# Last projection of a two-block transformer kernel: products ordered by token tile and by half of the contraction, final norm by tile, store in four parts

## Chip, core and metric

The kernel runs as one program on one core of a Trainium2 chip. The metric is device time in microseconds (us), the median of the runs; lower is better. The engines named below are TensorE (PE in the rows; PEld is its weight load), VectorE (DVE), ScalarE (ACT), GpSimd (POOL) and SyncE (SP), which here issues nearly all DMAs.

## What is computed

256 tokens of width 1024 pass through two blocks in float32. The first is a gated recurrence beside latent attention and then a mixture of 64 experts; the second has three attentions (moba, dsa, cross), a gated merge of their outputs and an output projection. Only the end of the second block matters here:

```python
def hybrid_layer(x, mem, ...):
    ...
    gates = jax.nn.sigmoid(glog + b_merge).reshape(B, S, N_BRANCH_2, D_MODEL)
    u = gates[:, :, 0] * ya + gates[:, :, 1] * yb + gates[:, :, 2] * yc
    return x + u @ w_out                      # u: 256 x 1024, w_out: 1024 x 1024

def rmsnorm_2(x, g):
    xf = x.astype(jnp.float32)
    y = xf * lax.rsqrt(jnp.mean(xf * xf, axis=-1, keepdims=True) + RMS_EPS)
    return (y * g.astype(jnp.float32)).astype(x.dtype)

# second_block returns rmsnorm_2(x, g_final)
```

## The kernel before

The 256 tokens are two tiles of 128 (NT = 2), and the width of 1024 is 8 pieces of 128 (KC = 8). `X` holds the residual stream with tokens on the partitions, `[128, 2, 1024]`. The order of all work is one list, `PLAN`, made by `plan()` and written out by hand. Each engine has its own program that walks this list and issues its own part of each step, so the order on an engine is the order of the list; between engines there are only semaphores.

Matrix products go to four regions of PSUM of 1024 columns: `P0` and `P1`, which the `proj` steps use in turn, and `A` and `B`. `full[r]` counts how often a region has been filled, `empty[r]` how often it has been read out. `may_fill` makes TensorE wait until the region's previous use was read. `USE` keeps these counts for each step.

The last steps of the list are `um0, um1, ud0, ud1, ux0, ux1` (the three branches' up-projections, feature-major, each half of the 1024 features: index 0 is features 0 to 511, index 1 features 512 to 1023), then `w20, w21` (the output projection, columns 0 to 511 and 512 to 1023) and `final`.

- After each `ux` step VectorE multiplies the result by its gate and adds it to `gl[0]`, two operations; the second frees the region. `gl[0]` is `u` transposed, `[128, 8, 256]`: pieces 0 to 3 are complete after `ux0`, 4 to 7 after `ux1`.
- `w20` and `w21` (`token_major`, L803 by way of `proj`) take a 128 x 128 piece of `gl[0]` as weights and 512 columns of `w_out` as the moving operand. Both wait until `ux0` and `ux1` have been read out (L932 to L935). Each does token tile 0 over the eight pieces, then token tile 1 over the eight. In float32 each product is two matmul records in the trace: 8 x 2 x 2 = 32 for each of `w20` and `w21`. One semaphore increment stands at the end of each.
- VectorE adds the region to `X`, both token tiles in one operation of 1024 columns (the line of `tt`, L1298).
- `final`: ScalarE squares both tiles with a sum over the row (L1099), loads the table of the square root and takes it (L1102). VectorE takes the reciprocal (L1305) and multiplies each tile by the root and by the gain row (L1681). SyncE then stores the whole output, 1 MB, with one DMA (L775), and waits for it.

Weights come into a ring of four slots; those of `w21` go to the slot of `um` and are issued when `um1` is done.

Of the kernel before, what the change touches and what calls it, by code (L numbers as in the profile page):

```python
# [141 lines left out]
def plan():  # L142
# [3 lines left out]
    def proj(*names):  # L146
        p.extend(("proj", n, "P") for n in names)
# [74 lines left out]
    turn(5, 9, "gl4")  # L222
    turn(9, 10, "gl5")
    turn(10, None, "um0", "um1")
    proj("ud0", "ud1", "ux0", "ux1", "w20", "w21")
    p.append(("final", 0, ""))
    return p


# [37 lines left out]
def build(nc, ins, out):  # L267
    with ExitStack() as ctx:
# [131 lines left out]
        def one_up(e, name):  # L400
            for s in ONE_UP[name]:
                e.sem_inc(s, 1)
        stored = sem("stored")

        block = ctx.enter_context(nc.Block())

# [303 lines left out]
        def _(sp):  # L710
# [60 lines left out]
                    sp.dma_start(wrow_f, ins["g_final_2"].unsqueeze(0).broadcast_to([P, D])).then_inc(row_in, 16)  # L771
                load(UNITS_2, n)

            sp.wait_ge(normed, 5)
            sp.dma_start(out[0].rearrange("(t p) d -> p t d", p=P), xo[:, :, :]).then_inc(stored, 16)  # L775
            sp.wait_ge(stored, 16)


        @block.gpsimd
# [8 lines left out]
        def _(pe):  # L788
            def transposes(key, src_of, region, n, done=True):
# [3 lines left out]
                    mm = pe.transpose(ps[region][:, i * P:(i + 1) * P], src_of(i), ident)  # L793
                mm.then_inc(full[region], 1)

            def proj(key, name, lhs_of, rhs_of, kc, outs):

                may_fill(pe, key)
                r = region_of(key)
                for o in range(len(outs(ps[r]))):  # L800
                    dst = outs(ps[r])[o]
                    for k in range(kc):
                        mm = pe.matmul(dst, lhs_of(o, k), rhs_of(o, k), start=(k == 0), stop=(k == kc - 1))  # L803
                mm.then_inc(full[r], 1)

            def rows_out(cols):
                return lambda z: [z[:, t * 512:t * 512 + cols] for t in range(NT)]
# [14 lines left out]
            rope_n = {"iq": 1, "ik": 1, "dq": 2, "dk": 3, "mq": 4, "mk": 5}  # L822

            for name, arg, _ in PLAN:
                key = (name, arg)
                if name == "norm":
                    if arg == "x":
# [49 lines left out]
                elif name == "proj":  # L877
# [23 lines left out]
                    elif arg in ("wa0", "wa1"):  # L901
                        if arg == "wa0":
                            wait_empty(pe, ("hg_outT", 0))
                        feature_major(key, arg, oaT)
                    elif arg in ("wb0", "wb1"):
                        if arg == "wb0":
                            wait_empty(pe, ("pv", 2))
                        feature_major(key, arg, obT)
                    elif arg == "wo0":
                        wait_empty(pe, ("proj", "wb0"))  # L910
                        wait_empty(pe, ("proj", "wb1"))
                        token_major(key, arg, Y)
                    elif arg in ("iq", "dq", "dk", "dv", "mq", "mk", "mv"):
                        if arg == "iq":
                            wait_empty(pe, ("norm", "mid"))
                        token_major(key, arg, hT)
                    elif arg == "ikw":
                        token_major(key, arg, hT, cols=72)
                    elif arg in ("xq", "mg", "dg", "xg") or arg[:2] == "gl":
                        feature_major(key, arg, hT)  # L920
                    elif arg == "xk":
                        wait_empty(pe, ("norm", "mem"))
                        feature_major(key, arg, memT)
                    elif arg == "xv":
                        token_major(key, arg, memT)
                    elif arg[0] == "u":
                        kind = {"m": "mg", "d": "dg", "x": "xg"}[arg[1]]
                        last = {"m": 8, "d": 5, "x": 10}[arg[1]]
                        if arg[2] == "0":
                            wait_empty(pe, ("pv", last))  # L930
                        feature_major(key, arg, sg[kind], kc=4, c0=512 * int(arg[2]))
                    elif arg in ("w20", "w21"):  # L932
                        if arg == "w20":
                            wait_empty(pe, ("proj", "ux0"))
                            wait_empty(pe, ("proj", "ux1"))  # L935
                        token_major(key, arg, gl[0])
                elif name == "level":
                    n = arg
# [142 lines left out]
        def _(act):  # L1081
# [31 lines left out]
            for name, arg, _ in PLAN:  # L1113
# [165 lines left out]
                elif name == "moe":  # L1279
                    rounds = moe_scalar(act)  # L1280
                elif name == "final":
                    wait_empty(act, ("proj", "w20"))
                    wait_empty(act, ("proj", "w21"))
                    square_sums(lambda t: X[:, t, :], lambda t: xo[:, t, :], 4, 48, D)


        @block.vector
        def _(dve):
# [68 lines left out]
            for name, arg, _ in PLAN:  # L1357
# [63 lines left out]
                elif name == "proj":  # L1421
# [36 lines left out]
                    elif arg == "wo1":  # L1458
# [1 line left out]
                        tt(X[:, 0, 512:D], ps[r][:, 0:512], X[:, 0, 512:D], ALU.add).then_inc(x_sum, 1)  # L1460
                        wait_full(dve, key)
                        tt(X[:, 1, 512:D], ps[r][:, 512:1024], X[:, 1, 512:D], ALU.add).then_inc(empty[r], 1)
                    elif arg in ("wo0", "w20", "w21"):
                        i = int(arg[2])
                        wait_full(dve, key)
                        x = tt(X[:, :, 512 * i:512 * i + 512], rows(ps[r]), X[:, :, 512 * i:512 * i + 512], ALU.add)
# [205 lines left out]
                elif name == "moe":  # L1672
                    rounds = experts(dve, link, tt)
                elif name == "final":

                    wait_empty(dve, ("proj", "w20"))
                    wait_empty(dve, ("proj", "w21"))
                    inverse_root(50)
                    dve.wait_ge(row_in, 32)
                    for t in range(NT):  # L1680
                        i = dve.scalar_tensor_tensor(out=xo[:, t, :], in0=X[:, t, :], scalar=small[:, 50 + t:51 + t],  # L1681
                                                     in1=wrow_f, op0=ALU.mult, op1=ALU.mult)
                    i.then_inc(normed, 1)

# [54 lines left out]
```

## Time and profile before

| | us |
|---|---|
| median of 3 runs | 1761.36 |
| lowest, highest | 1760.98, 1761.41 |
| the profiled execution's own time | 1762.46 |
| its span in the profile | 1760.6 |
| PE busy | 1384.9 (79%) |
| DVE busy | 329.5 (19%) |
| ACT busy | 209.0 (12%) |

The span runs from the first to the last instruction that the profiler recorded; the 1.86 us between it and the execution's own time lie around it. "Busy" is a share of the whole span and says little about one stage: the expert stage, from about 430 to 1350 us, is bound by its weights' transfers, and the end of the program by a chain of single instructions. The chain that ended last (below) gives for each step what released it. The granted clock is the share of TensorE's full 2.4 GHz that it was given in a stretch: 1.00 is 2.4 GHz, 0.50 is 1.2 GHz, and a value between them is a mean over both.

### The profile page before, as it was taken

The page shows a single profiled execution, that of the slowest core. Times are in us where ns is not written, and L with a number is a line of the kernel's source. Part 1 is how long each engine was busy: PE and PEld are TensorE (multiplying, and loading weights), DVE is VectorE, ACT ScalarE, POOL GpSimd, SP SyncE. Part 2 cuts the span into 40 slices and gives each one's busy share as a digit, 9 for nine tenths or more (in the row PEclk, how much of TensorE's full clock was granted, in tenths as well). Part 3 has the DMA queues.
Part 4 walks back from the last instruction along what each step waited for, and adds up shares of the span by engine and source line. Part 5 has one row for each costly group of instructions (what it writes and reads, how often), then busy time and mean ns, then how long its engine had stood idle before and what let it go on. Part 6 is the DMA issues. An engine that isn't in the chain of part 4 may idle for free.

```text
span 1760.6 us, 16409 instructions
## 1 busy us (share of the span) xinstructions
PE 1384.9 (79%) x7184; PEld 778.7 (44%) x7184; DVE 329.5 (19%) x585; ACT 209.0 (12%) x366; POOL 1.4 (0%) x6
## 2 busy tenths in 40 slices
PE   6999989888866676656666666666667999999996
PEld 5756886775322122212221222122214546788882
DVE  2233432312211001101010101010101221252221
ACT  1000032202000000000000000000001001143300
POOL 0000000000000000000000000000000000000000
PEclk9999998988987788878887888888878999999998
DMA  7324133317999999999999999999997433332310
GB/s 285 114 103 172 67 117 146 102 51 330 394 429 433 433 431 429 433 434 432 429 430 435 433 429 430 435 433 430 430 435 337 171 134 137 132 144 108 142 50 24
DMA packets 24550, 504.43 MB, mean 287 GB/s; under 512 B 4672, under 2 KB 4928, under 8 KB 6336
## 3 DMA queue, kind: packets, MB, share of 16 engines
q1 hardware_dynamic: 24080, 503.69, 68.6%
q8 instruction: 30, 0.49, 0.1%
q10 hardware_dynamic: 432, 0.17, 0.0%
q14 instruction: 8, 0.07, 0.0%
HBM read 502.81 MB, written 1.05 MB: 286 GB/s over the span
## 4 chain that ended last, share of the span: by engine, by line
PE 51%; DMA 44%; DVE 3%; ACT 1%; issue 1%; SPq 0%; DVEq 0%; ACTq 0%
DMA arena<-in_experts 44%; PE psP L803 35%; PE psP L481 5%; PE psP L492 3%; DVE arena L1298 2%; PE psB L1064 1%; PE psB L793 1%; PE psA L948 1%; PE psB L948 1%; PE psA L1030 1%; PE psA L1029 1%; PE psA L793 0%; PE psA L502 0%; PE psP L848 0%; PE psP L842 0%
## 5 line engine op out<-in xcount | busy, mean ns | idle before, releaser
L803 PE MATMUL psP<-arena,ring 128*128 128x256 f32 x1664 | 369.3, 384 | 2.2 <-DVE arena L1298 1.4
L803 PEld LDWEIGHTS psP<-arena,ring 128*128 128x128 f32 x1664 | 319.1, 193 | 48.1 <-issue 4.2
L481 PE MATMUL psP<-ring,arena 128*32 128x512 f32 x1024 | 162.1, 792 | 103.9 <-DMA ring<-in_experts 103.9
L803 PE MATMUL psP<-ring,arena 128*128 128x512 f32 (+2 forms) x576 | 233.1, 564 | 7.3 <-DVE arena L1298 7.3
L481 PE MATMUL psP<-arena 128*32 128x512 f32 x1024 | 158.1, 774 | 99.8 <-DMA arena<-in_experts 99.8
L1298 DVE TENSOR_TENSOR X<-X,psA 128x512 f32<-128x512 f32 x68 | 46.8, 688 | 682.1 <-PE psA L502 682.1
L803 PEld LDWEIGHTS psP<-ring,arena 128*128 128x128 f32 x576 | 105.7, 191 | 126.1 <-issue 126.0
L481 PEld LDWEIGHTS psP<-ring,arena 128*32 128x32 f32 x1024 | 41.0, 139 | 223.2 <-issue 176.5
L481 PEld LDWEIGHTS psP<-arena 128*32 128x32 f32 x1024 | 37.3, 136 | 217.9 <-DMA arena<-in_experts 126.5
L492 PE MATMUL psP<-arena 128*32 128x512 f32 x512 | 76.8, 754 | 53.6 <-DMA arena<-in_experts 49.8
L492 PE MATMUL psP<-ring,arena 128*32 128x512 f32 x512 | 73.4, 725 | 48.0 <-DMA ring<-in_experts 44.5
L467 PEld LDWEIGHTS psA<-arena 128*128 128x128 f32 x544 | 64.0, 197 | 15.1 <-issue 15.1
L502 PE MATMUL psA<-arena 128*128 128x512 f32 x136 | 67.4, 618 | 2.0 <-ACT arena L578 1.2
L467 PE MATMUL psA<-arena 128*128 128x128 f32 x544 | 67.2, 283 | 1.2 <-DVE small L627 1.2
L492 PEld LDWEIGHTS psP<-arena 128*32 128x32 f32 x512 | 18.1, 134 | 106.4 <-DMA arena<-in_experts 61.8
L1298 DVE TENSOR_TENSOR arena<-arena 128x1024 f32<-128x1024 f32 (+6 forms) x90 | 63.1, 729 | 1.2
L492 PEld LDWEIGHTS psP<-ring,arena 128*32 128x32 f32 x512 | 17.9, 129 | 97.9 <-issue 46.7
L1108 ACT ACTIVATE arena<-psP 128x1024 f32<-128x1024 f32 (+1 forms) x26 | 26.1, 1002 | 286.7 <-PE psP L803 286.7
L571 ACT ACT_TABLE_LOAD x16 | 20.5, 1283 | 276.6 <-PE psP L481 276.6
L573 ACT ACTIVATE arena<-psB 128x256 f32<-128x256 f32 x16 | 6.1, 383 | 333.3 <-PE psB L542 333.3
L578 ACT ACTIVATE arena<-psP 128x1024 f32<-128x1024 f32 x16 | 16.4, 1023 | 244.2 <-PE psP L492 244.2
L502 PEld LDWEIGHTS psA<-arena 128*128 128x128 f32 x136 | 23.0, 189 | 48.4 <-issue 44.6
(223 smaller groups left out, 748.3 us busy)
## 6 DMA issues: line engine op xcount, KB each, us to landing
arena<-in_experts SPq DMA_DIRECT2D x48, 4096.0 KB, 33.3
ring<-in_experts SPq DMA_DIRECT2D x48, 4096.0 KB, 33.3
ring<-in_u_gl SPq DMA_DIRECT2D x6, 2048.0 KB, 7.7
ring<-in_u_hf SPq DMA_DIRECT2D x2, 2048.0 KB, 11.9
ring<-in_u_hq SPq DMA_DIRECT2D x2, 2048.0 KB, 22.0
ring<-in_u_hv SPq DMA_DIRECT2D x2, 2048.0 KB, 7.7
ring<-in_u_hg SPq DMA_DIRECT2D x2, 2048.0 KB, 7.4
ring<-in_u_ga SPq DMA_DIRECT2D x2, 2048.0 KB, 7.5
```

The lines of the kernel that those rows point to most:

```text
L467: mm = pe.matmul(zA[:, k * P:(k + 1) * P], xnf[:, t, k * P:(k + 1) * P], selA[:, t].rearrange("p j c -> p (j c)"), start=(t == 0), stop=(t ...
L481: mm = pe.matmul(z[j * CAP:(j + 1) * CAP, :], x[:, 4 * half + k, j * CAP:(j + 1) * CAP], held[c % 4][:, j, k * 512:(k + 1) * 512], start=( ...
L492: mm = pe.matmul(zY[j * CAP:(j + 1) * CAP, cols * 512:(cols + 1) * 512], hidT[:, 2 * half + f, j * CAP:(j + 1) * CAP], held[c % 4][:, j, f ...
L502: pe.matmul(zA[:, c:c + 512], selTs[:, t * P:(t + 1) * P], ysb[:, half * 512:(half + 1) * 512], start=True, stop=True).then_inc(scattered, 1)
L571: act.activation(gs, ps["P0"][:, 0:512], ACT.Silu).then_inc(gate_read, 1)
L793: mm = pe.transpose(ps[region][:, i * P:(i + 1) * P], src_of(i), ident)
L803: mm = pe.matmul(dst, lhs_of(o, k), rhs_of(o, k), start=(k == 0), stop=(k == kc - 1))
L948: mm = pe.matmul(ps[r][:, h * P:(h + 1) * P], k[:, h, t * P:(t + 1) * P], q[:, h, t * P:(t + 1) * P], start=True, stop=True)
L1029: pe.matmul(dst, qn[:, h, tt], kn[:, h, 0:nk], start=True, stop=False)
L1030: mm = pe.matmul(dst, qpeT[lo:lo + 64, h // 2, tt], kpeT[lo:lo + 64, 0:nk], start=False, stop=True)
L1108: act.activation(dst, view(ps[r]), func, **kw).then_inc(empty[r], 1)
L1298: return dve.tensor_tensor(o, a, b, op)
```

## The change

The last projection is issued in six pieces in place of two. A new kind of step, `("head", (name, upto), "")`, makes TensorE issue the products of `name` up to number `upto` (piece by piece of the contraction, tile 0 first), and `begun` remembers how far a step has come. Tile 0 is done first, in four pieces: `w20` over features 0 to 511, `w21` over the same, then `w20` and `w21` over features 512 to 1023. Only the pieces with features 512 to 1023 wait for `ux1`. Then come `w20` and `w21` for tile 1.

`final` is a step of its own for each tile; that of tile 0 stands ahead of tile 1's products in the list. Each adds, squares, normalises and multiplies in halves of 512 columns, and VectorE adds the two sums of squares before ScalarE takes the root. A root of a constant is taken at the start of `final` 0 and has no use for its value. The output is stored with four DMAs of 128 rows by 512 columns (256 KB each), each as soon as its part is written.

```diff
--- before.py
+++ after.py
@@ -222,8 +222,12 @@
     turn(5, 9, "gl4")
     turn(9, 10, "gl5")
     turn(10, None, "um0", "um1")
-    proj("ud0", "ud1", "ux0", "ux1", "w20", "w21")
+    proj("ud0", "ud1", "ux0", "ux1")
+    p.extend([("head", ("w20", 4), ""), ("head", ("w21", 4), ""), ("head", ("w20", 8), ""), ("head", ("w21", 8), "")])
     p.append(("final", 0, ""))
+    proj("w20", "w21")
+    p.append(("final", 1, ""))
     return p
@@ -401,6 +405,8 @@
             for s in ONE_UP[name]:
                 e.sem_inc(s, 1)
         stored = sem("stored")
+        w2_tile, x_done, x_squared, x_rooted, x_out = (sem(n) for n in ("w2_tile", "x_done", "x_squared", "x_rooted", "x_out"))
+        final_sums = sem("final_sums")
         block = ctx.enter_context(nc.Block())
@@ -771,9 +777,11 @@
                     sp.dma_start(wrow_f, ins["g_final_2"].unsqueeze(0).broadcast_to([P, D])).then_inc(row_in, 16)
                 load(UNITS_2, n)
-            sp.wait_ge(normed, 5)
-            sp.dma_start(out[0].rearrange("(t p) d -> p t d", p=P), xo[:, :, :]).then_inc(stored, 16)
-            sp.wait_ge(stored, 16)
+            for n, (t, half) in enumerate(((0, 0), (0, 1), (1, 0), (1, 1))):
+                part = slice(512 * half, 512 * half + 512)
+                sp.wait_ge(x_out, n + 1)
+                sp.dma_start(out[0, t * P:(t + 1) * P, part], xo[:, t, part]).then_inc(stored, 16)
+            sp.wait_ge(stored, 64)
         @block.gpsimd
@@ -793,15 +801,23 @@
                     mm = pe.transpose(ps[region][:, i * P:(i + 1) * P], src_of(i), ident)
                 mm.then_inc(full[region], 1)
+            begun = {}
             def proj(key, name, lhs_of, rhs_of, kc, outs):
-                may_fill(pe, key)
                 r = region_of(key)
-                for o in range(len(outs(ps[r]))):
-                    dst = outs(ps[r])[o]
-                    for k in range(kc):
-                        mm = pe.matmul(dst, lhs_of(o, k), rhs_of(o, k), start=(k == 0), stop=(k == kc - 1))
-                mm.then_inc(full[r], 1)
+                dsts = outs(ps[r])
+                if name not in begun:
+                    may_fill(pe, key)
+                stop_at = upto or len(dsts) * kc
+                for i in range(begun.get(name, 0), stop_at):
+                    o, k = i // kc, i % kc
+                    mm = pe.matmul(dsts[o], lhs_of(o, k), rhs_of(o, k), start=(k == 0), stop=(k == kc - 1))
+                begun[name] = stop_at
+                if name in ("w20", "w21") and stop_at == kc:
+                    mm.then_inc(w2_tile, 1)
+                if stop_at == len(dsts) * kc:
+                    mm.then_inc(full[r], 1)
             def rows_out(cols):
                 return lambda z: [z[:, t * 512:t * 512 + cols] for t in range(NT)]
@@ -822,6 +838,10 @@
             rope_n = {"iq": 1, "ik": 1, "dq": 2, "dk": 3, "mq": 4, "mk": 5}
             for name, arg, _ in PLAN:
+                upto = None
+                if name == "head":
+                    name, (arg, upto) = "proj", arg
                 key = (name, arg)
                 if name == "norm":
                     if arg == "x":
@@ -930,9 +950,7 @@
                             wait_empty(pe, ("pv", last))
                         feature_major(key, arg, sg[kind], kc=4, c0=512 * int(arg[2]))
                     elif arg in ("w20", "w21"):
-                        if arg == "w20":
-                            wait_empty(pe, ("proj", "ux0"))
-                            wait_empty(pe, ("proj", "ux1"))
+                        wait_empty(pe, ("proj", "ux0" if upto == 4 else "ux1"))
                         token_major(key, arg, gl[0])
                 elif name == "level":
                     n = arg
@@ -1279,9 +1297,17 @@
                 elif name == "moe":
                     rounds = moe_scalar(act)
                 elif name == "final":
-                    wait_empty(act, ("proj", "w20"))
-                    wait_empty(act, ("proj", "w21"))
-                    square_sums(lambda t: X[:, t, :], lambda t: xo[:, t, :], 4, 48, D)
+                    t = arg
+                    if t == 0:
+                        act.activation(small[:, 236:237], eps, ACT.Sqrt)
+                    for half in range(2):
+                        act.wait_ge(x_done, 2 * t + half + 1)
+                        x = act.activation(xo[:, t, 512 * half:512 * half + 512], X[:, t, 512 * half:512 * half + 512], ACT.Square,
+                                           accum_out=small[:, 48 + 2 * t + half:49 + 2 * t + half])
+                    x.then_inc(x_squared, 1)
+                    act.wait_ge(final_sums, t + 1)
+                    act.activation(small[:, 54 + t:55 + t], small[:, 52 + t:53 + t], ACT.Sqrt, bias=eps, scale=1.0 / D).then_inc(x_rooted, 1)
         @block.vector
@@ -1460,7 +1486,12 @@
                         tt(X[:, 0, 512:D], ps[r][:, 0:512], X[:, 0, 512:D], ALU.add).then_inc(x_sum, 1)
                         wait_full(dve, key)
                         tt(X[:, 1, 512:D], ps[r][:, 512:1024], X[:, 1, 512:D], ALU.add).then_inc(empty[r], 1)
-                    elif arg in ("wo0", "w20", "w21"):
+                    elif arg in ("w20", "w21"):
+                        i = int(arg[2])
+                        wait_full(dve, key)
+                        part = X[:, 1, 512 * i:512 * i + 512]
+                        tt(part, ps[r][:, 512:1024], part, ALU.add).then_inc(x_done, 1)
+                    elif arg in ("wo0",):
                         i = int(arg[2])
                         wait_full(dve, key)
                         x = tt(X[:, :, 512 * i:512 * i + 512], rows(ps[r]), X[:, :, 512 * i:512 * i + 512], ALU.add)
@@ -1672,15 +1703,21 @@
                 elif name == "moe":
                     rounds = experts(dve, link, tt)
                 elif name == "final":
-                    wait_empty(dve, ("proj", "w20"))
-                    wait_empty(dve, ("proj", "w21"))
-                    inverse_root(50)
-                    dve.wait_ge(row_in, 32)
-                    for t in range(NT):
-                        i = dve.scalar_tensor_tensor(out=xo[:, t, :], in0=X[:, t, :], scalar=small[:, 50 + t:51 + t],
-                                                     in1=wrow_f, op0=ALU.mult, op1=ALU.mult)
-                    i.then_inc(normed, 1)
+                    t = arg
+                    if t == 0:
+                        for i in range(2):
+                            dve.wait_ge(w2_tile, i + 1)
+                            part = X[:, 0, 512 * i:512 * i + 512]
+                            tt(part, ps[region_of(("proj", f"w2{i}"))][:, 0:512], part, ALU.add).then_inc(x_done, 1)
+                        dve.wait_ge(row_in, 32)
+                    dve.wait_ge(x_squared, t + 1)
+                    tt(small[:, 52 + t:53 + t], small[:, 48 + 2 * t:49 + 2 * t], small[:, 49 + 2 * t:50 + 2 * t], ALU.add).then_inc(final_sums, 1)
+                    dve.wait_ge(x_rooted, t + 1)
+                    link(dve.reciprocal(small[:, 56 + t:57 + t], small[:, 54 + t:55 + t]))
+                    for half in range(2):
+                        part = slice(512 * half, 512 * half + 512)
+                        dve.scalar_tensor_tensor(out=xo[:, t, part], in0=X[:, t, part], scalar=small[:, 56 + t:57 + t],
+                                                 in1=wrow_f[:, part], op0=ALU.mult, op1=ALU.mult).then_inc(x_out, 1)
```

How the order of the instructions changes is shown at two places. The first is TensorE at the end of its program: before, from `ud0` on (`128x256` are the up-projections, `128x512` are `w20` in `psP1` and `w21` in `psP0`).

```order
L803 MATMUL psP1<-arena,ring 128x256 x16
L803 MATMUL psP0<-arena,ring 128x256 x16
L803 MATMUL psP1<-arena,ring 128x256 x16
L803 MATMUL psP0<-arena,ring 128x256 x16
L803 MATMUL psP1<-ring,arena 128x512 x16
L803 MATMUL psP0<-ring,arena 128x512 x16
```

And now, from `ux0` on, where the line of the matmul is 815:

```order
L815 MATMUL psP1<-arena,ring 128x256 x16
L815 MATMUL psP0<-arena,ring 128x256 x16
L815 MATMUL psP1<-ring,arena 128x512 x4
L815 MATMUL psP0<-ring,arena 128x512 x4
L815 MATMUL psP1<-ring,arena 128x512 x4
L815 MATMUL psP0<-ring,arena 128x512 x4
L815 MATMUL psP1<-ring,arena 128x512 x8
L815 MATMUL psP0<-ring,arena 128x512 x8
```

The number of products is the same, 32; the first four rows of four are tile 0, the last two tile 1. Only what they wait for and where they signal differs.

The second place is VectorE at the end of its program: before, from the second operation of `ux1` (`psP1` and `psP0` are `w20` and `w21`, `small` the norm's columns, `arena<-X,small,arena` the output).

```order
L1298 TENSOR_TENSOR arena<-arena 128x1024
L1298 TENSOR_TENSOR X<-psP1,X 128x2x512
L1298 TENSOR_TENSOR X<-psP0,X 128x2x512
L1305 RECIPROCAL small<-small 128x2
L1681 SCALAR_TENSOR_TENSOR arena<-X,small,arena 128x1024 x2
```

And now, from the same operation; L1324 is the line of `tt`:

```order
L1324 TENSOR_TENSOR arena<-arena 128x1024
L1324 TENSOR_TENSOR X<-psP1,X 128x512
L1324 TENSOR_TENSOR X<-psP0,X 128x512
L1324 TENSOR_TENSOR small<-small 128x1
L1716 RECIPROCAL small<-small 128x1
L1719 SCALAR_TENSOR_TENSOR arena<-X,small,arena 128x512 x2
L1324 TENSOR_TENSOR X<-psP1,X 128x512
L1324 TENSOR_TENSOR X<-psP0,X 128x512
L1324 TENSOR_TENSOR small<-small 128x1
L1716 RECIPROCAL small<-small 128x1
L1719 SCALAR_TENSOR_TENSOR arena<-X,small,arena 128x512 x2
```

The chain of the norm stands there twice, each on half the rows, and the first one stands ahead of the two additions of tile 1.

## Rows read from the trace of the kernel before

**Rows 1.** The page, part 4: the chain that ended last, by engine.

```profile
PE 51%; DMA 44%; DVE 3%; ACT 1%; issue 1%; SPq 0%; DVEq 0%; ACTq 0%
```

**Rows 2.** Chain of waits in order of time, 1716 to 1749 us: start, us, what.

```profile
1716.12 1.23 DVE arena L1298
...
1717.38 1.24 DVE arena L1298
...
1718.86 29.41 PE psP L803 x64
...
1748.30 1.24 DVE X L1298
```

**Rows 3.** Timeline of the end, all engines: start, us, engine, line, operation, [idle before].

```profile
1749.62 1.06 ACT L1099 ACTIVATE arena<-X 128x1024 f32<-128x1024 f32 x1 [77.33 <-DVE X L1298]
1750.58 0.19 ACT L1099 ACTIVATION_READ_ACCUMULATOR arena<-X 128x1 f32 x1
...
1751.82 1.28 ACT L1102 ACT_TABLE_LOAD   x1
1753.12 0.29 ACT L1102 ACTIVATE small<-small,consts_sb 128x2 f32<-128x2 f32 x1
1753.55 0.17 DVE L1305 RECIPROCAL small<-small 128x2 f32<-128x2 f32 x1 [4.02 <-ACT small L1102]
1753.75 2.48 DVE L1681 SCALAR_TENSOR_TENSOR arena<-X,small,arena 128x1024 f32<-128x1024 f32 x2
1756.26 0.39 SPq L775 DMA_DIRECT2D out<-arena  x1
```

**Rows 4.** Timeline: ux0's last operation, w21's weight load, ux1's last matmul.

```profile
1686.70 0.33 SPq L725 DMA_DIRECT2D ring<-in_u_w  x1
...
1710.48 1.23 DVE L1298 TENSOR_TENSOR arena<-arena 128x1024 f32<-128x1024 f32 x1
...
1715.71 0.38 PE L803 MATMUL psP<-arena,ring 128*128 128x256 f32 x1
```

**Rows 5.** Windows around the gap: us, busy (x) by engine, PEclk, DMA, GB/s.

```profile
1718.80:1722.50 3.70, 3.64 (x5) 1.60 (x6) 0.00 (x0) 0.00 (x0) 0.00 (x0) 0.54 0.00 0
1722.50:1748.30 25.80, 25.77 (x61) 11.06 (x59) 1.23 (x1) 0.00 (x0) 0.00 (x0) 1.00 0.00 0
```

**Rows 6.** Timeline of PE, weight loads of the last projection: first and last of 34.

```profile
1733.08 0.19 PEld L803 LDWEIGHTS psP<-ring,arena 128*128 128x128 f32 x1 [0.24 <-issue]
...
1747.24 0.19 PEld L803 LDWEIGHTS psP<-ring,arena 128*128 128x128 f32 x1 [0.24 <-issue]
```

**Rows 7.** Timeline of PE, 370 to 412 us: the first block's output projection.

```profile
391.99 13.97 PE L803 MATMUL psP<-ring,arena 128*128 128x512 f32 x32 [2.78 <-DVE arena L1298]
```

**Rows 8.** Timeline, 412 to 425 us: the first block's norm, same forms.

```profile
412.87 0.69 DVE L1298 TENSOR_TENSOR X<-psP,X 128x512 f32<-128x512 f32 x1 [4.98 <-PE psP L842]
...
421.77 0.63 ACT L1143 ACTIVATE arena<-X 128x512 f32<-128x512 f32 x1 [3.56 <-DVE X L1298]
422.31 0.19 ACT L1143 ACTIVATION_READ_ACCUMULATOR arena<-X 128x1 f32 x1
...
423.83 0.15 DVE L1298 TENSOR_TENSOR small<-small 128x2 f32<-128x2 f32 x1
...
424.01 0.30 ACT L1146 ACTIVATE small<-small,consts_sb 128x2 f32<-128x2 f32 x1 [1.52 <-DVE small L1298]
...
424.34 0.17 DVE L1668 RECIPROCAL small<-small 128x2 f32<-128x2 f32 x1 [0.36 <-ACT small L1146]
```

**Rows 9.** DMA issues: out<-in, count, KB each, us to landing.

```profile
ring<-in_u_w SPq DMA_DIRECT2D x2, 2048.0 KB, 7.8
...
out<-arena SPq DMA_DIRECT2D x1, 1024.0 KB, 4.0
```

**Rows 10.** Windows inside the store, columns as in Rows 5.

```profile
1757.00:1757.20 0.20, 0.00 (x0) 0.00 (x0) 0.00 (x0) 0.00 (x0) 0.00 (x0) 0.50 0.37 143
...
1759.60:1759.80 0.20, 0.00 (x0) 0.00 (x0) 0.00 (x0) 0.00 (x0) 0.00 (x0) 0.50 0.78 307
```

## The prediction

> **What bounds the kernel now.** I read the chain that ended last first, since a sum of busy times says nothing about so late a change. By engine it is PE 51% and DMA 44% of the span [rows 1]; the DMA share is the expert stage, which is not touched. So only the end of the chain counts, and there I read it in order of time [rows 2]: VectorE's two operations of `ux1` (1.23 us each, from 1716.12), then one stretch of 64 matmul records of `w20` and `w21` (29.41 us from 1718.86), then VectorE's addition at 1748.30. The timeline of what follows [rows 3] is a row of single instructions, none beside another: squares of two tiles, a table load, a root, a reciprocal, two products, one store. From the last product (1718.86 + 29.41 = 1748.27) to the end of the span (1760.6) that is 12.3 us in which TensorE does nothing. Two things can be won: time ahead of and inside the stretch of products, and time in these 12.3 us. Whatever else is moved lies beside TensorE's work and costs nothing.
>
> **Part 1, the start of `w20`.** Before, TensorE stands still between `ux1`'s last matmul, which starts at 1715.71 [rows 4], and 1718.86, since the first product of `w20` waits for both `ux` steps to be read out. Now the first four pieces need only `ux0`, whose last operation on VectorE starts at 1710.48 and takes 1.23, so it was free at 1711.71 [rows 4], 4 us before it is asked for. The weights of `w21` were issued at 1686.70 [rows 4] and such a load lands after 7.8 us [rows 9], so they are no wait. In the same stretch weight loads follow each other at (1747.24 - 1733.08) / 33 = 0.429 us [rows 6], half of that for half as many columns, so the first record of `w20` starts about 0.2 after the last one of `ux1`, at 1715.9. Gain 1718.86 - 1715.9 = 2.96. The next wait is close: `w21`'s first half goes to the region that `ux1`'s second operation frees, at 1717.38 + 1.24 = 1718.62 [rows 2]. It comes after 8 records, at 1715.9 + 8 x 0.429 = 1719.3. So it is 0.7 us clear of it, and the later halves, which read what `ux1` wrote, start 3.4 us later still. If that margin were gone TensorE would stand for the difference only, some tenths.
>
> **Part 2, the clock behind the gap.** Windows: in the 3.70 us from 1718.80 the granted clock is 0.54, in the 25.80 us after it 1.00 [rows 5]. So the first products ran nearly all at the lower of the two levels, 1.2 GHz, after 2.8 us of standing still, and that lost 3.70 x (1 - 0.54) = 1.7 us. Without the gap TensorE goes from `ux1` into `w20` without a pause. I count the 1.7 whole. The other end is 0: a gap of the same 2.78 us ahead of the first block's output projection was followed by 32 records in 13.97 us [rows 7], that is at full speed (31 x 0.429 = 13.3, and the last one's own time), so gap and lower clock are not tied one to one in this kernel, and a fall that comes for another reason would stay. A loss beyond that is the rival below. The products end at 1748.27 - 2.96 - 1.7 = 1743.6. That there are six waits in place of two I put at nothing: at the border of `w20` and `w21` there is one now, inside the stretch of rows 6, and the weight loads keep their step of 0.429 across it.
>
> **Part 3, tile 0 behind tile 1's products.** Tile 0 is complete after 32 of the 64 records, at 1715.9 + 32 x 0.429 = 1729.6 plus the last one's own time. Then come, in this order, half an addition, half a square, sum, root, reciprocal, two halves of the output and two stores, some 4 us of instructions, and the stores. Tile 1 takes TensorE until 1743.6, so all of it has 13 us of cover. On VectorE the two additions of tile 1 are queued behind this chain; the first of them is wanted at 1743.6 - 16 x 0.429 = 1736.7, when the chain has ended for 3 us or so. On SyncE only the stores are left. ScalarE had nothing to do for 77.33 us ahead of the squares [rows 3], so the early root and the table load before it (1.28) are hidden there; what they take away is the load in the tail. Without the cover, part 3 would cost its own 4 us.
>
> **Part 4, the tail that is left.** From the last product on, durations from the same forms in the first block's norm [rows 8], where an instruction starts 0.03 after what it waited for:
> - addition of 512 columns: 0.03 + 0.69 = 0.72
> - square of 512 with its sum: 0.03 + (422.31 - 421.77) + 0.19 = 0.76. The first half is done already, 6.9 us earlier.
> - sum of two columns: 0.03 + 0.15 = 0.18
> - root, now without a table load: 0.03 + 0.30 = 0.33
> - reciprocal: 0.03 + 0.17 = 0.20
> - two output products of 512. The whole one takes 2.48 / 2 = 1.24 in step [rows 3]. Halving costs more than half: an addition takes 1.23 with 1024 columns [rows 2] and 0.69 with 512, so 0.15 is fixed. Two halves: 1.28 - 0.54 = 0.74 each, less 0.1 of overlap, and 0.03: 1.4
> - the last store: from 0.03 after, see below, 2.0
> - from landing to the end of the span: 1760.6 - (1756.26 + 4.0) = 0.34
>
> For the store the windows show the parts [rows 3, 9, 10]: issued at 1756.26, first data at about 1757.1 (the window from 1757.00 has a DMA share of 0.37), last at about 1759.76, landed at 1760.26. So 0.84 before and 0.50 behind the data are fixed, and 2.66 are for 1024 KB. A quarter moves in 0.66, and 0.84 + 0.66 + 0.50 = 2.0. The store before it is issued 0.65 earlier, so its data are gone just when these start. Bounds: a quarter of 4.0, that is 1.0, if nothing were fixed; 4.0, that of the whole store, if a smaller one is no quicker or four of them get in each other's way. I take 2.0, which the windows of this very store give.
>
> Sum 0.72 + 0.76 + 0.18 + 0.33 + 0.20 + 1.43 + 2.03 + 0.34 = 6.0. In the tail of now two handovers took longer than 0.03 (0.09 from VectorE's addition to the square, 0.14 from the root to the reciprocal, [rows 2, 3]), so I take 6.1. That is 12.3 - 6.1 = 6.2 less.
>
> The Trainium skill (page "DMA: Bandwidth & Descriptors", section "Anatomy of one DMA") has a line for this: a DMA takes about 2.0 us fixed plus its bytes over 436 GB/s, and further down it advises transfers of 1 MiB and more, which speaks against four stores of 256 KB. For the whole store it gives 4.4 where the trace has 4.0; for a quarter it gives 2.6, and the estimate would be 0.6 higher, 1751.1. Its page "ScalarE: Activation LUTs" (section "What ACT_TABLE_LOAD costs") puts a switch of tables at 2.66 us with a drain of 1.38 beside the load. Here the root starts 0.02 after the load's end (1751.82 + 1.28, 1753.12) [rows 3], so the trace does not agree for this place, and 1.3 is what goes.
>
> **Sum.** 2.96 + 1.7 + 6.2 = 10.9 us. The profiled execution took 1762.46 us, 1.86 beside its span of 1760.6; the new span is 1749.7. The median of the runs is 1761.36, 1.1 under the profiled execution; the same saving gives 1761.36 - 10.9 = 1750.5.
>
> **The rivals.**
> - The lower clock comes anyway. For it: [rows 7], where the same gap had no fall behind it, so something besides the gap decides. Against it: all the work from 1722.5 to 1748.3 at 1.00, and a program that is the same up to `ux1`. Then 1750.5 + 1.7 = 1752.2. Chance 0.12.
> - The small stores are no quicker: the fourth waits behind the third, or its fixed part is larger than I read. With 4.0 in place of 2.0: 1752.5; with one more fixed part of 1.34 only, 1751.8. For it: nothing in this trace is a store of this size. Against it: the data of the whole store moved at 1.05 MB in 2.66 us and only 1.34 us lay beside them. The advice on large transfers cited above would make the same. Chance 0.13.
> - The change does not do what it says at the front: `w20` still waits for `ux1`, by a wait on a region or by an order that I misread. Then only the tail is won, 1761.36 - 6.2 = 1755.2. Against it: `ux0` and `w20` share `psP1`, and `ux1` and `w21` `psP0`. Chance 0.02.
> - Slower than before: TensorE now works from 1671 to 1743.6 without the pause of 2.8 us, and the chip grants less in the end of such a stretch. The products of `w20` and `w21` are 27 us at full speed; all of them at 1.2 GHz would cost 27 more, 1777.5. It turns the sign once 10.9 us of work run at the lower level. For it: the clock did fall once in this place. Against it: the fall came behind the pause and the 25.8 us of work after it ran at 1.00 [rows 5]. Chance 0.01.
>
> **How the numbers follow.** The forecast has the remaining 0.72, with its own range 1749.5 (store at 1.0) to 1751.3 (handovers of 0.1 at each of five places, the store at 2.5). The range of 8 in 10 has to take in the first two rivals: 1749.3 to 1752.7. A measurement of this kernel tells a change of over 0.2%, 3.5 us, from none: that is below 1757.8. All cases but the last lie below it; faster 0.98, same 0.01, slower 0.01.
>
> **What would show it.** In the changed profile: no idle of TensorE between the `128x256` and `128x512` matmuls and 64 records in 27.6 us with a clock of 1.00; if they take 29, part 2 is wrong; if the first starts near 1718.9, part 1. The addition, square, sum, root, reciprocal and two stores of tile 0 between 1730 and 1736, and the second addition of tile 1 right at the products' end, or part 3 is wrong. No table load behind the products, and 6.1 us from the last product to the end of the span. The last of four stores lands 2.0 us after its issue; 2.6 or more would show the fixed part mis-sized. The forecast falls as a whole if the time is above 1752.7 with the same time up to `ux1`.

## Result: 1748.5 us, 2.0 us below the forecast and outside its range

| | before | changed |
|---|---|---|
| median of the first comparison (4 runs each) | 1761.17 | 1748.50 (1748.20 to 1749.30) |
| the same again (18 and 5 runs) | 1761.07 (1759.76 to 1762.40) | 1749.82 (1748.55 to 1750.58) |
| span of the profiled execution | 1760.6 | 1747.5 |
| its own time | 1762.46 | 1749.30 |

The ratio is 0.993 with a 95% interval of 0.9919 to 0.9942, in the second comparison 0.9935 (0.9922 to 0.9949). The forecast was 1750.5, with a range from 1749.3 to 1752.7. The sign and the mechanism held. The size did not: 12.7 us were won in the first comparison, where the sum said 10.9; in the second it was 11.2. The profiled execution of the kernel before (1762.46) is not among the runs of either median; those of the changed kernel are.

The chain of waits of the changed kernel, in order of time (start, us, what), from the last stretch of TensorE on; it answers to [rows 2, 3]:

```profile
1689.96 51.44 PE psP L815 x175
...
1741.42 0.70 DVE X L1324
...
1742.15 0.73 ACT arena L1306 x2
...
1742.90 0.17 DVE small L1324
...
1743.10 0.30 ACT small L1310
...
1743.42 0.17 DVE small L1716
...
1743.62 0.75 DVE arena L1719
1744.38 0.66 DVEq L272
```

TensorE's work is now one piece without a wait from `ux0` to the end of `w21`. Behind it each step of the tail stands within 0.02 of the duration that was forecast (0.69, 0.73, 0.15, 0.30, 0.17). The span ends 1747.5 - 1741.39 = 6.1 after the last product.

The stretch of the 64 records, from the timeline of all engines, with tile 0's work beside it:

```profile
1713.76 27.63 PE L815 MATMUL psP<-ring,arena 128*128 128x512 f32 x64
...
1715.22 1.23 DVE L1324 TENSOR_TENSOR arena<-arena 128x1024 f32<-128x1024 f32 x1
1724.26 0.69 DVE L1324 TENSOR_TENSOR X<-psP,X 128x512 f32<-128x512 f32 x1 [7.82 <-PE psP L815]
...
1727.69 0.69 DVE L1324 TENSOR_TENSOR X<-psP,X 128x512 f32<-128x512 f32 x1 [2.74 <-PE psP L815]
...
1729.96 1.42 DVE L1719 SCALAR_TENSOR_TENSOR arena<-X,small,arena 128x512 f32<-128x512 f32 x2
1730.74 14.66 SPq L783 DMA_DIRECT2D out<-arena  x4
```

The first product starts 1.46 ahead of `ux1`'s second operation, where before it started 1.48 behind it (1718.86 against 1717.38, [rows 2]): 2.94 won. The 64 records take 27.63, before 29.40: 1.77 won. Tile 0's chain is over at 1731.4, 3.2 us before VectorE's addition for tile 1 at 1734.56. The DMA view gives the four stores (KB each, median us to landing):

```profile
out<-arena SPq DMA_DIRECT2D x4, 256.0 KB, 2.0
```

Together 2.94 + 1.77 + (12.34 - 6.11) = 10.94, the 10.9 of the sum. The same from one point that the change doesn't touch, the issue of `w20`'s weights, to the end of the span. Before it was

```profile
1666.20 20.84 SPq L725 DMA_DIRECT2D ring<-in_u_w  x2
```

and 1760.6 - 1666.20 = 94.40 (the line holds both issues; [rows 4] shows the later one, for `w21`), and now it is

```profile
1664.03 0.33 SPq L731 DMA_DIRECT2D ring<-in_u_w  x1
```

1747.5 - 1664.03 = 83.47: 10.93 less. So the other 2.2 us of the 13.1 between the two spans lie ahead of 1664 us, where the two programs are alike. Followed back by the starts of VectorE's instructions, the difference of 2.2 us is there at 33 us already (35.52 against 33.27 for the first instruction behind the projection) and, apart from swings within the expert stage, stays. It lies in the first projection. Here are the windows from 18 to 20 us. The columns are those of [rows 5]: the first busy time is TensorE's, with its number of matmuls in brackets. Before:

```profile
18.00:20.00 2.00, 1.86 (x5) 1.53 (x6) 1.53 (x9) 0.21 (x1) 0.00 (x0) 1.00 1.03 442
```

and in the changed kernel:

```profile
18.00:20.00 2.00, 1.95 (x9) 1.78 (x10) 1.44 (x8) 0.21 (x1) 0.00 (x0) 1.00 0.99 426
```

5 matmuls against 9 in the same time. The column of the granted clock reads 1.00 in both, but it can't have been the full one in the first, where equal matmuls came at half the rate: the trace has a record of the clock only from 22.5 us on, and the other from 16.8 us on, and what is printed ahead of the first record is no measurement. Where the clock is unknown, the spacing of equal instructions is the measure.

### The profile page after: what moved, and what is told of

Same layout as the page of the kernel before. It is cut to its first block, busy times and chain, and to the rows that moved or that the text cites. A ratio compares the mean times of both kernels' runs of the same rounds, so it can differ in the third digit from the quotient of the medians.

```text
span 1747.5 us, 16426 instructions
## 1 busy us (share of the span) xinstructions
PE 1377.8 (79%) x7184; PEld 777.6 (44%) x7184; DVE 330.8 (19%) x592; ACT 210.2 (12%) x372; POOL 1.4 (0%) x6
## 4 chain that ended last, share of the span: by engine, by line
PE 51%; DMA 44%; DVE 3%; ACT 1%; issue 1%; SPq 0%; DVEq 0%; ACTq 0%
DMA arena<-in_experts 44%; PE psP L815 35%; PE psP L487 5%; PE psP L498 3%; DVE arena L1324 2%; PE psB L1082 1%; PE psB L801 1%; PE psA L966 1%; PE psB L966 1%; PE psA L1048 1%; PE psA L1047 1%; PE psA L801 0%; PE psA L508 0%; PE psP L868 0%; PE psP L862 0%
## 5 line engine op out<-in xcount | busy, mean ns | idle before, releaser
L487 PE MATMUL psP<-ring,arena 128*32 128x512 f32 x1024 | 159.2, 779 | 104.9 <-DMA ring<-in_experts 104.9
L1324 DVE TENSOR_TENSOR X<-X,psA 128x512 f32<-128x512 f32 x68 | 46.8, 688 | 682.8 <-PE psA L508 682.8
L498 PE MATMUL psP<-ring,arena 128*32 128x512 f32 x512 | 72.5, 718 | 48.4 <-DMA ring<-in_experts 44.9
L1324 DVE TENSOR_TENSOR arena<-arena 128x1024 f32<-128x1024 f32 (+6 forms) x90 | 63.1, 730 | 1.2
L584 ACT ACTIVATE arena<-psP 128x1024 f32<-128x1024 f32 x16 | 16.4, 1023 | 242.7 <-PE psP L498 242.7
```

The lines of the kernel that those rows point to most:

```text
L487: mm = pe.matmul(z[j * CAP:(j + 1) * CAP, :], x[:, 4 * half + k, j * CAP:(j + 1) * CAP], held[c % 4][:, j, k * 512:(k + 1) * 512], start=( ...
L498: mm = pe.matmul(zY[j * CAP:(j + 1) * CAP, cols * 512:(cols + 1) * 512], hidT[:, 2 * half + f, j * CAP:(j + 1) * CAP], held[c % 4][:, j, f ...
L1324: return dve.tensor_tensor(o, a, b, op)
```

## Experiments

There are twelve experiments, two with the unchanged kernels and ten with variants. The first two settle whether the start is a property of the program or of the execution.

**e1, e2: both kernels again, unchanged.**

> The kernel before, unchanged. What is at stake is the start of the program: the first projection began at 18.1 us in both traces, but in the trace of before its first ten matmuls came at half the rate and in that of the changed kernel at the full one, and 2.2 us of the difference between the two spans lie there. Theory 1, the start differs by chance from execution to execution: this trace may show the full rate from 18.1 us, and the times scatter by up to 2 us. Theory 2, the start belongs to the built program: the trace shows the half rate until 22.5 us again, and all times lie within 0.6 us of each other and around 1761.2.

> The changed kernel, unchanged. Theory 1, chance: times scatter over 2 us, and the start may be at half rate. Theory 2, the start belongs to the program: full rate from 18.1 us again, all times around 1748.5, ratio 0.993. In both the end from the last product is 6.1 us.

Measured: 1760.83 (1759.28 to 1762.40, 11 runs) and 1749.82 (1748.55 to 1750.58). The windows from 18 to 20 us of the second trace of the changed kernel (its projection starts at 18.40):

```profile
18.00:20.00 2.00, 1.60 (x4) 1.36 (x5) 1.53 (x9) 0.21 (x1) 0.00 (x0) 1.00 0.96 410
```

The very program that had the quick start now has the slow one: 4 matmuls. So theory 2 is out; the start differs from execution to execution. The issue of the load for `hv`, which waits for the first projection, is a point in time that shows it. In four timelines of SyncE, first before, e1 and e2:

```profile
34.39 0.33 SPq L725 DMA_DIRECT2D ring<-in_u_hv  x1
```

```profile
34.27 0.33 SPq L725 DMA_DIRECT2D ring<-in_u_hv  x1
```

```profile
34.05 0.33 SPq L731 DMA_DIRECT2D ring<-in_u_hv  x1
```

and the first trace of the changed kernel:

```profile
32.13 0.33 SPq L731 DMA_DIRECT2D ring<-in_u_hv  x1
```

Over the ten traces of kernels whose start is unchanged, this issue lies between 34.0 and 34.4 in six (before, e1, e2, e3, e9, e11) and between 31.7 and 32.1 in four (changed, e4, e7, e8). From `w20`'s weights to the end e2 takes 1748.8 - 1665.36 = 83.44 and e1 1760.6 - 1666.18 = 94.42, each equal to the first trace of its kernel within the 0.1 to which the spans are given. The 1.92 us between the two traces of the changed kernel (34.05 against 32.13) are not the rate alone: in e2 the projection also starts 0.35 later (18.40 against 18.05). And they are 1.33 at `w20`'s weights (1665.36 against 1664.03). Averaged over the ten traces, the two groups are 2.3 us apart at the load for `hv` and 2.5 at `w20`'s weights, so on the whole the difference is kept; between the two points the ten traces differ by up to 0.7 us for other reasons.

**e3: only the order of the products.** The edit that matters, as a difference to the changed kernel:

```diff
-    p.append(("final", 0, ""))
     proj("w20", "w21")
-    p.append(("final", 1, ""))
+    p.append(("final", 0, ""))
```

Additions, norm and store are those of the kernel before.

> Only the new order of the products (tile 0 first, by halves of the contraction); additions, norm and the one store of 1 MB as before. By the sum on record 2.96 for the wait and 1.7 for the clock: 4.7 less than before, from the second ux step on. In all, theory 1 (start by chance): 4.7 plus or minus 2. Theory 2 (start of the program): 4.7, or 6.9 if this program too starts at the full rate.

Measured: 1756.63 (8 runs), ratio 0.9972 (0.9961 to 0.9983), 4.4 less. The timeline of TensorE has the whole gain of parts 1 and 2, and the end from the last product is 12.37, that of before; from `w20`'s weights to the end it is 4.7 less than before, as in the sum:

```profile
1715.60 27.63 PE L812 MATMUL psP<-ring,arena 128*128 128x512 f32 x64
```

**e4: only the end,** as a difference to the changed kernel.

```diff
-                        wait_empty(pe, ("proj", "ux0" if upto == 4 else "ux1"))
+                        wait_empty(pe, ("proj", "ux0"))
+                        wait_empty(pe, ("proj", "ux1"))
```

> The changed kernel, but w20 waits for both ux steps as before, so that the gap of 2.8 us stays and only the end is new. By the sum on record 6.2 less than before from the first product of w20 on, 64 records in 29.4 us if the clock falls behind the gap and in 27.6 if not. In all 6.2, or 8.4 with a start at the full rate.

Measured: 1754.16 (5 runs), ratio 0.9964 (0.995 to 0.9977), 6.9 less. The end is 6.06; gap and lower clock are back, as the timeline of TensorE shows:

```profile
1715.59 29.35 PE L815 MATMUL psP<-ring,arena 128*128 128x512 f32 x64 [2.78 <-DVE arena L1325]
```

From `w20`'s weights to the end e4 takes 6.3 less than before. With the 4.7 of e3 that makes 11.0, against 10.9 for the whole change, so the parts add up. The medians say the same more roughly, since each carries its own starts (the profiled execution of e4 is one with the quick start): 4.4 and 6.9 against 1761.07 - 1749.82 = 11.2.

**e9: the wait without the standing still,** in the kernel before.

```diff
                         if arg == "w20":
+                            for _ in range(11):
+                                pe.matmul(ps["A"][:, 0:P], ident, ident, start=True, stop=True)
                             wait_empty(pe, ("proj", "ux0"))
```

> The kernel before, with 11 products of 128 x 128 of the identity into a region that is free and not read again, while TensorE waits for ux1 ahead of w20. The wait stays, the standing still goes. If the lower clock behind the gap comes from standing still (1.7 us of the sum on record): the 64 records take 27.6 us in place of 29.4, 1.8 less than before in the end. If it comes for another reason: 29.4, no change.

Measured: 1758.50 (11 runs), ratio 0.9989 (0.998 to 0.9998), 2.3 less. TensorE in this trace:

```profile
1715.22 2.62 PE L935 MATMUL psA<-consts_sb 128*128 128x128 f32 x22
1718.00 27.70 PE L803 MATMUL psP<-ring,arena 128*128 128x512 f32 x64 [0.17 <-issue]
```

From `w20`'s weights to the end it takes 1.8 less than before; the median says 2.3, with an interval that nearly reaches no change. Products that nobody reads take away 1.70 us of the stretch behind them. So here the lower clock did come from the standing still, and the 1.7 of the sum was no chance of one trace: the 64 records take 29.3 to 29.4 us in the four traces with the gap (before, e1, e4, e5) and 27.63 in the nine without it.

That a gap of this length is always followed by a lower clock does not hold. The same gap of 2.78 us ahead of the first block's output projection [rows 7] is in all fourteen traces. In twelve of them the 32 records behind it take 13.97 us; in e5 and e12 they take 15.6:

```profile
386.56 15.64 PE L819 MATMUL psP<-ring,arena 128*128 128x512 f32 x32 [2.78 <-DVE arena L1331]
```

Up to that point e12 has the same instructions as e10, which is one of the twelve, so at that place it differs from execution to execution. What decides there is not shown.

**e7: one store.**

```diff
-            for n, (t, half) in enumerate(((0, 0), (0, 1), (1, 0), (1, 1))):
-                ...
+            sp.wait_ge(x_out, 4)
+            sp.dma_start(out[0].rearrange("(t p) d -> p t d", p=P), xo[:, :, :]).then_inc(stored, 16)
```

> The changed kernel with one store of 1 MB behind the last output product in place of four. By the windows of the store (0.84 and 0.50 us fixed, 2.66 us of data) 2.0 more in the end: 8.1 us from the last product to the end of the span in place of 6.1. By the rival (small stores no quicker) 6.1. By the Trainium skill's line of 2.0 us and 436 GB/s 1.8 more.

Measured: 1750.82 (5 runs), against the 1749.82 of e2, whose starts may differ. The end from the last product is 8.03 in place of 6.1: 1.93 more, where 2.0 was expected, and the store lands after 4.0 us again where the small ones take 2.0. The Trainium skill (page "DMA: Bandwidth & Descriptors", section "Anatomy of one DMA") gives about 2.0 us plus the bytes over 436 GB/s for a DMA that GpSimd issues; this store is issued by SyncE. The estimate of the difference by its rate, 1.8, is close to the 1.93; its fixed part doesn't fit, since the windows of the store [rows 10] leave 1.34 beside the data.

**e8: a table load in the end.**

```diff
                     act.activation(small[:, 54 + t:55 + t], ..., ACT.Sqrt, ...).then_inc(x_rooted, 1)
+                    if t == 0:
+                        act.activation(small[:, 237:238], eps, ACT.Exp)
```

> The changed kernel, and on ScalarE an exponential of a constant behind tile 0's root, which is hidden; it puts a table load ahead of tile 1's root, into the end. The load can start when the square is done, while VectorE adds the two sums (0.2 us). By the rows of before: 1.28 - 0.2 = 1.1 more in the end, 7.2 us from the last product. By the drain that the Trainium skill counts with a switch, 1.38 more: 8.5. If the load is done ahead of the squares' wait: 6.1.

Measured: 1750.45 (5 runs); the end is 7.17, 1.07 more. Timeline of the end:

```profile
1741.82 0.19 ACT L1306 ACTIVATION_READ_ACCUMULATOR arena<-X 128x1 f32 x1
1742.03 1.28 ACT L1310 ACT_TABLE_LOAD   x1
1742.04 0.16 DVE L1326 TENSOR_TENSOR small<-small 128x1 f32<-128x1 f32 x1 [0.79 <-ACT arena L1306]
1743.32 0.29 ACT L1310 ACTIVATE small<-small,consts_sb 128x1 f32<-128x1 f32 x1
```

The load runs beside VectorE's sum and costs 1.28 less these 0.2. The root starts 0.01 after the load's end and the load 0.02 after the square's sum is read, so nothing of the 1.38 more that the expectation set against it shows.

**e5, e6: 80 products of zeros at the start,** on the kernel before and on the changed one.

```diff
+            pe.wait_ge(warm_in, 1)          # GpSimd has cleared the tile
+            for _ in range(80):
+                pe.matmul(ps["P1"][:, 0:P], warm[:, :], warm[:, :], start=True, stop=True)
```

> The kernel before, and ahead of its first transposes 80 products of 128 x 128 of zeros into a region that nobody reads, while TensorE would wait for the input anyway. Theory 1 (the clock comes up at a different time after the first work in each execution, between 15.7 and 22.5 us so far): now it is up before 13 us in every execution, the transposes take 1.1 in place of 1.9 us each, the first projection runs at the full rate from its start. Time 1761.1 less 1.4 to 1.7 for the transposes and the addition between, less 0 to 2.2 for the projection: 1757.5 to 1759.5, and a narrower scatter than 2.6 us if the start is all of it. Theory 2 (scatter from elsewhere, such as the transfers of the expert stage): time 1759.5, scatter as wide as before. Rival: 80 products delay the transposes: slower.

> The changed kernel with the same 80 products at the start. Both theories: 11.0 less than the kernel before with them. Theory 1: 1746.3 to 1748.3 and a narrow scatter; theory 2: 1748.3, as wide as before. The end from the last product is 6.1 us.

Measured: 1766.55 and 1756.12 (5 and 8 runs), 5.8 and 6.3 slower than without. The rival that the products delay the transposes came true; I had counted them at too quick a pace. The timeline of TensorE in e5:

```profile
1.00 19.95 PE L829 MATMUL psP<-warm 128*128 128x128 f32 x160 [1.00 <-POOL warm L784]
...
20.78 1.04 PE L796 MATMUL psA<-consts_sb,arena 128*128 128x128 f32 x8
```

160 records at 0.125 us are 20 us, and the transposes start 7.7 us late. Eight records of them take 1.04 in place of the 1.94 that they took before, so the clock is up. The times still scatter over 2.8 and 2.3 us, so the start is not all of the scatter.

**e10: the same with 44, on the changed kernel.**

> The changed kernel with 44 products of zeros at the start (80 took 20 us and delayed the transposes by 7.7 us; at their 0.125 us a record 44 take 11 and end before the input is ready). Theory 1 (the start's clock carries the scatter of the spans): clock up before 13 us, first projection from 16.7 us at the full rate, the weights of hv asked for at about 30.6 in place of 32.1 or 34.2; time 1749.8 less 1.4 to 3.6, about 1747. Rival: later waits give it back, 1749.8.

Measured: 1747.81 (1747.01 to 1748.85, 5 runs), ratio 0.9928 (0.9914 to 0.9941), 2.0 less than e2 and 1.3 less than the median of all nine runs of the changed kernel. TensorE's start:

```profile
1.00 11.64 PE L845 MATMUL psP<-warm 128*128 128x128 f32 x88 [1.00 <-POOL warm L792]
13.00 1.07 PE L804 MATMUL psA<-consts_sb,arena 128*128 128x128 f32 x8 [0.36 <-DVE arena L1394]
...
16.68 13.62 PE L818 MATMUL psP<-arena,ring 128*128 128x256 f32 x62 [1.74 <-DVE arena L1330]
```

The load for `hv` is issued at 30.76 and the span is 1745.4. From `w20`'s weights (1661.94) on it is 83.46 once more. These weights are issued earlier than in any of the ten traces without the products (1662.92 to 1666.20), so later waits don't take the gain back in this trace. By the medians alone it is not settled: the intervals of the ratios of e10 and e2 (0.9922 to 0.9949) overlap, and the two ran in different comparisons. The scatter is 1.8 us over five runs, as in e2 (2.0): the start is not all of it.

**e11, e12: one more gap.** In the changed kernel TensorE still stands still for 2.13 us at 1666 us:

```profile
1667.91 1.11 PE L801 MATMUL psB<-consts_sb,arena 128*128 128x128 f32 x8 [2.13 <-DVE arena L1324]
```

Here `um0` is issued ahead of the last `probsT`; e12 has the 44 products too.

```diff
-    turn(10, None, "um0", "um1")
+    turn(10, None, "um1", ahead=("um0",))     # proj(*ahead) stands before ("probsT", g, "B")
```

> The changed kernel with um0's products issued ahead of the last probsT, where TensorE stands still for 2.13 us and runs 3.4 us at the lower clock behind it. The same two effects as in the change itself: 2.1 and 1.7 less, 3.8 in all, 1746.0, if VectorE's order (um0 behind pv) does not hold the regions. Rival: um1's region or the softmax's evacuation comes late and a gap opens elsewhere: 1748 or more.

> The changed kernel with the start of e10 and the order of e11: their gains are in different stages, so about 1743.5 if both hold; ratio to the kernel before 0.990.

Measured: 1746.85 (5 runs), ratio 0.9916 (0.9903 to 0.993), and 1743.08 (1742.93 to 1745.24, 4 runs), ratio 0.9903 (0.9888 to 0.9919). In e11 TensorE has no idle there:

```profile
1665.72 1.95 PE L1083 MATMUL psB<-arena 128*128 128x128 f32 x16
1667.51 7.07 PE L816 MATMUL psP<-arena,ring 128*128 128x256 f32 x32
1674.42 1.04 PE L802 MATMUL psB<-consts_sb,arena 128*128 128x128 f32 x8
1675.29 7.07 PE L816 MATMUL psP<-arena,ring 128*128 128x256 f32 x32
```

From `w20`'s weights on it takes 1745.3 - 1665.92 = 79.4 in place of 83.45, 4.1 less than the changed kernel, where 3.8 was expected. The medians of e11 and e2 are 3.0 apart. e12 is the fastest version found, 18 us below the kernel before.

## Why the prediction was wrong

- **Part 1, 2.96:** measured 2.94 in the first trace, and e3 has it without the new end. Right. The wait of `w21` on `ux1`'s region did not show.
- **Part 2, 1.7:** measured 1.77, and the same 1.7 in e9 by other means. Right; the rival of a clock that falls anyway did not come about in any of the nine traces without the gap. The doubt that [rows 7] raised was justified all the same: at that other place the same gap cost 1.6 to 1.7 in two traces of fourteen.
- **Part 3, nothing:** right. The chain of tile 0 ended 3.2 us before VectorE was wanted.
- **Part 4, 6.2:** measured 6.23 (12.34 to 6.11). Right, with the store at 2.0 and no table load. e7 puts 1.93 on the split of the store, e8 1.07 on the table load. The rival of stores that are no quicker is out, and so are 2.6 us for a quarter.
- **The sum, 10.9:** measured 10.93 between the issue of `w20`'s weights and the end. Right.
- **The step from the sum to the time: this failed.** It reads "The median of the runs is 1761.36, 1.1 under the profiled execution; the same saving gives 1761.36 - 10.9 = 1750.5", and below it "a program that is the same up to `ux1`". I took the time up to `ux1` as fixed: neither the sum nor the range has a term for what executions differ by ahead of it, and that was put at nothing because three runs of before lay within 0.43 us. Eighteen runs lie within 2.6. One cause could be shown: the first projection runs at half rate for up to 4.4 us in some executions and not in others, and the traces of the two kinds are 2.3 us apart behind it and 2.5 at `w20`'s weights. The profiled execution of before had the half rate and that of the changed kernel had not, which makes 2.2 of the 13.1 us between the two spans. The nine runs of the changed kernel have a median of 1749.07; three of the first four lie below my range and three of the five later ones within it, 1749.82 to 1750.58. So it was partly chance that the first comparison fell outside: the median of the second lies within the range. By these scatters a range for a median of a few runs had to be about 1 us wider on both sides than the terms of the sum made it; that is an estimate.

What stays open: the rest of the scatter. One of twelve later runs of the kernel before took 1764.31, 2.1 us above the next. With the 44 products ahead of the transposes, and the clock up by then in the one profiled execution of each, the times of e10 still spread over 1.8 us and those of e12 over 2.3; where it arises in executions that were not profiled can't be seen. That the first four runs of the changed kernel all had a quick start is likely from their median but not shown, since one of them was profiled.

## What to carry to other kernels

Sum a change from the nearest point of the program that it does not touch, here the issue of a load, and compare two traces from there: it separated 10.9 us of effect from 2.2 us of start. Before a forecast is given to a tenth of a per cent, ask what an execution may differ by ahead of that point, and don't read the scatter from three runs. A gap of TensorE costs its own length and can cost a stretch at the lower clock behind it (1.7 us here, in every trace at one place and in two of fourteen at another), so filling it, be it with products for nobody, can pay even where the wait stays; but count such products by their own pace, 0.12 to 0.13 us a record here.

## What the runs showed that I had not expected

- The same program starts at the full or at half the rate: 9 or 4 matmuls of 128 x 256 between 18 and 20 us. The spans of the two are 1.3 us apart; for the traces of before and changed the start makes 2.2 us.
- The printed clock is 1.00 ahead of the first record of it, whatever the true one.
- Small products of 128 x 128 took 0.125 us a record at the start, where the pace of those in the attention stage was 0.11 (16 from 1665.72 to 1667.51, where the next ones start, in e11).
- A store of 256 KB lands 2.0 us after its issue, one of 1 MB 4.0 (e7 and before); that the end took the 6.1 us of the sum leaves no room for one of two stores issued 0.66 us apart to have held up the other.
